# Output projection and MLP of a decoder step: unrolled, smaller weight groups, token scale applied to the relu output

## The reference, cut to what matters

```python
ob  = diff_head_norm(diff_attention(...), subln_gain, lambda_init)   # rmsnorm over 128 values of each head
mix = concatenate([oa, ob], axis=-1)                                 # 1024 per token
h   = x + mix @ w_out                                                # 1024 x 1024
u   = rmsnorm(h, norm_mlp) @ w_up                                    # 1024 x 4096
h   = h + square(relu(u)) @ w_down                                   # 4096 x 1024
y   = rmsnorm(h, final_norm)
```

## Time and profile before

| | us |
|---|---|
| runs (3): median, lowest, highest | 4612.5, 4608.19, 4615.78 |
| the profiled execution: span | 4601.9 |
| of it up to the stage `mlp` (its first transfer is issued at 2681.7) | 2681 |
| PE busy, share of the span | 4152.4, 90% |
| DVE | 2403.4, 52% |
| ACT | 1536.3, 33% |
| POOL | 805.8, 18% |

### The profile page before, as it was taken

One profiled execution on the slowest core, in us unless ns is written; L12 is line 12 of the kernel. 1 busy time (PEld: TensorE's weight loads), 2 busy tenths in 40 slices (PEclk: granted clock), 3 DMA queues, 4 the chain that ended last, 5 costly groups with the idle time before them and its releaser, 6 DMA issues. The chain is left out here.

```text
span 4601.9 us, 72420 instructions
## 1 busy us (share of the span) xinstructions
PE 4152.4 (90%) x22272; PEld 3160.3 (69%) x22272; DVE 2403.4 (52%) x5184; ACT 1536.3 (33%) x2569; POOL 805.8 (18%) x694
## 2 busy tenths in 40 slices
PE   7996998999989897888888879999999998999998
PEld 6875884445444444445444458988988997998898
DVE  3333334756677684444444435565565555555654
ACT  2221224555545443223322332233223223223322
POOL 0001000000000000333333322222222222222121
PEclk9997999999999998999999989999999999999999
DMA  5756623110111103999999953324333333332231
GB/s 187 234 194 211 228 76 86 36 37 8 36 35 37 36 10 114 376 330 350 365 348 349 360 171 120 116 95 128 127 100 113 124 110 103 125 118 99 94 125 61
DMA packets 347208, 686.79 MB, mean 149 GB/s; under 512 B 27769, under 2 KB 185465, under 8 KB 343610
## 3 DMA queue, kind: packets, MB, share of 16 engines
q1 hardware_dynamic: 291295, 448.03, 29.3%
q0 software_dynamic: 47488, 218.01, 13.3%
q10 hardware_dynamic: 8155, 17.77, 1.4%
HBM read 632.85 MB, written 117.70 MB: 163 GB/s over the span
## 5 line engine op out<-in xcount | busy, mean ns | idle before, releaser
L1379 POOL TENSOR_TENSOR d_up_lo<-d_up_raw,d_up_hi 128x2048 fp32r<-128x2048 f32 x100 | 460.6, 4606 | 1420.3 <-ACT d_up_hi L1516 1420.3
L1384 PE MATMUL d_ups<-d_a_hi,d_up_hi 128*128 128x416 f32 x1600 | 568.2, 355 | 16.9 <-DVE d_a_lo L1671 16.2
L1386 PE MATMUL d_ups<-d_a_hi,d_up_lo 128*128 128x416 f32 x1600 | 566.1, 354 | 0.0
L836 POOL DMA_DIRECT2D c_v<-in_v_cache x512 | 275.2, 537 | 1638.9 <-issue 1627.8
L1385 PE MATMUL d_ups<-d_a_lo,d_up_hi 128*128 128x416 f32 x1600 | 560.6, 350 | 0.0
L530 PE MATMUL b_s<-b_k,b_q 128*128 128x512 f32 (+3 forms) x1280 | 498.5, 547 | 54.1 <-DVE b_part L662 30.6
L1384 PE MATMUL d_dps<-d_u_hi,d_down_hi 128*128 128x416 f32 x1280 | 461.7, 361 | 57.6 <-DVE d_y L1696 55.8
L1696 DVE TENSOR_TENSOR d_y<-d_y,d_dps 128x416 f32<-128x416 f32 x640 | 367.9, 584 | 225.6 <-PE d_dps L1386 223.6
L1386 PE MATMUL d_dps<-d_u_hi,d_down_lo 128*128 128x416 f32 x1280 | 458.2, 358 | 0.0
L1385 PE MATMUL d_dps<-d_u_lo,d_down_hi 128*128 128x416 f32 x1280 | 454.0, 355 | 0.0
L530 PEld LDWEIGHTS b_s<-b_k,b_q 128*128 128x128 f32 x1280 | 236.6, 197 | 291.0 <-issue 191.1
(11 more groups left out here) (164 smaller groups left out, 6306.4 us busy)
## 6 DMA issues: line engine op xcount, KB each, us to landing
c_k<-in_k_cache SPq DMA_DIRECT2D x512, 256.0 KB, 6.2
c_v<-in_v_cache POOLq DMA_DIRECT2D x512, 256.0 KB, 5.7
d_down_raw<-in_w_down SPq DMA_DIRECT2D x80, 1024.0 KB, 5.1
d_up_raw<-in_w_up SPq DMA_DIRECT2D x80, 1024.0 KB, 7.3
out_ka_win<-in_ka_state POOLq DMA_DIRECT2D x8, 4064.0 KB, 14.6
out_va_win<-in_va_state POOLq DMA_DIRECT2D x8, 4064.0 KB, 26.5
d_up_raw<-in_w_out SPq DMA_DIRECT2D x20, 1024.0 KB, 7.5
a_x<-in_x_prompt SPq DMA_DIRECT2D x32, 512.0 KB, 4.1
```

The lines of the kernel that those rows point to most:

```text
L836: eng.dma_start(dst[i][:, g, :], io[src[0]][bass.ds(page, 1)].rearrange("o p d -> (o p) d")).then_inc(landed[i], 16)
L1379: nc.gpsimd.tensor_tensor(up_lo[i][:], up_raw[i][:], up_hi[i][:].bitcast(F32), ALU.subtract).then_inc(up_lo_ready, 1)
L1384: nc.tensor.matmul(dst, w_hi, x_hi, start=first, stop=False)
L1386: return nc.tensor.matmul(dst, w_lo, x_hi, start=False, stop=last)
```

## The change

All of `mlp` is straight code; no loop is left. In the new source the three matmuls are L1416 to L1418.

- Column groups of w_out and w_up are 128 wide (512 KB, rows of 512 bytes), with three buffers of `up_hi` and `up_lo` (UB). Groups are numbered through: 8 of w_out and 32 of w_up per block. Groups of w_down stay at 256 rows.
- `mix_hi`, `mix_lo` and `h_hi`, `h_lo` are separate. `mix` itself holds half a block at a time (4 chunks) and x a quarter. Mix and heads of the next block are prepared in groups MIX_AT = 3 and on and HEAD_AT = 8 and on.
- The up projection takes h times the gain. The token scale `per_token` = 1 / (mean square + eps) is the square of the norm's scale; DVE multiplies the relu output by it and then by the relu output. ACT makes the cast of u.
- POOL adds the squares of the 8 chunks (`add_square`), PE sums once (`sum_squares`) between the tiles up(0,0) and up(0,1).
- After a block each token tile of 104 is transposed, ACT squares it along its free dimension with an accumulated sum, and DVE multiplies by the token's scale and the gain row. SP stores.

On DVE, the end of a block before the change: down_lo and the split of group 15 stand ahead of the adds of group 14, head norms between them.

The diff, cut to its core:

```diff
-    GC = 256
-    NF = GC // P
-    OG, UG = D // GC, FF // GC
-    SG = OG + UG
+    NF = 2
+    OG, UG = KC, FF // (NF * P)
+    CG = OG + UG * NF
     NH = NP
-    DB = 3
+    UB, DB = 3, 3
+    XB = 2
+    MIX_AT, HEAD_AT, X_AT = 3, 8, 12
...
-        up_raw = [sb(f"d_up_raw{i}", [P, KC, GC]) for i in range(2)]
-        up_hi = [sb(f"d_up_hi{i}", [P, KC, GC], F32R) for i in range(2)]
-        up_lo = [sb(f"d_up_lo{i}", [P, KC, GC], F32R) for i in range(2)]
+        up_raw = [sb(f"d_up_raw{i}", [P, KC, P]) for i in range(2)]
+        up_hi = [sb(f"d_up_hi{i}", [P, KC, P], F32R) for i in range(UB)]
...
+                    b, s = n // CG, n % CG
+                    name, g = ("w_out", s) if s < OG else ("w_up", s - OG)
+                    src = io[name].rearrange("(c p) n -> p c n", p=P)[:, :, g * P:(g + 1) * P]
+                    sp.dma_start(up_raw[n % 2][:], src).then_inc(up_in[n % 2], 16)
...
+                    for c in range(KC):
+                        load_cols(out_no(b, c) + 2)
+                        if c % XB == 0 and 2 <= c // XB + 1 < KC // XB:
+                            load_x(b, c // XB + 1)
+                    for g in range(UG):
+                        load_cols(up_no(b, g, 0) + 2)
+                        load_rows(b, g)
+                        load_cols(up_no(b, g, 1) + 2)
...
-                        nc.gpsimd.tensor_tensor(up_lo[i][:], up_raw[i][:], up_hi[i][:].bitcast(F32),
-                                                ALU.subtract).then_inc(up_lo_ready, 1)
+                def cols_lo(n):
+                    if n >= NB * CG:
+                        return
+                    pool.wait_ge(up_hi_ready, n + 1)
+                    nc.gpsimd.tensor_tensor(up_lo[n % UB][:], up_raw[n % 2][:], up_hi[n % UB][:].bitcast(F32),
+                                            ALU.subtract).then_inc(up_lo_ready, 1)
...
+                    if c == 1:
+                        wait(pool, summed, b)
+                        nc.gpsimd.tensor_tensor(squares[:], square[:, 0, :], square[:, 1, :], ALU.add).then_inc(sq_added, 1)
+                    elif c > 1:
+                        pool.wait_ge(sq_added, b * (KC - 1) + c - 1)
+                        nc.gpsimd.tensor_tensor(squares[:], squares[:], square[:, c % 2, :], ALU.add).then_inc(sq_added, 1)
...
+                for b in range(NB):
+                    for c in range(KC):
+                        cols_lo(out_no(b, c) + 2)
+                        if c:
+                            add_square(b, c - 1)
+                    cols_lo(up_no(b, 0, 0) + 2)
+                    add_square(b, KC - 1)
...
-                def add_square(first, last):
-                    if first:
...
-                        pe.wait_ge(square_used, n)
-                        pe.sem_inc(s_full, 1)
...
+                def sum_squares(b):
+                    pe.wait_ge(sq_added, (b + 1) * (KC - 1))
+                    pe.wait_ge(head_rooted, (b + 1) * NH)
+                    nc.tensor.matmul(s_ps[:, 0:W], ones[:], squares[:], start=True, stop=True).then_inc(summed, 1)
...
-                        if c >= 2:
-                            add_square(c == 2, False)
-                    add_square(False, False)
-                    add_square(False, True)
-                    if b:
-                        for c in range(KC):
-                            add_square(c == 0, c == KC - 1)
...
-                    down(b, UG - 2, 0, (lambda c: c % 2 and add_square(True, True)) if b + 1 < NB else lambda c: None)
-                    down(b, UG - 1, 1)
...
+                    for g in range(UG + 1):
+                        if g < UG:
+                            up(b, g, 0)
+                            if g == 0:
+                                sum_squares(b)
+                            up(b, g, 1)
...
+                                    wait(pe, y_ready, 2 * y_no(b - 1, t))
+                                turn_y(b - 1, t, half, t_ps[half])
+                            if b < LAST and HEAD_AT < g <= HEAD_AT + NH and c == 4:
+                                sum_head(b + 1, g - HEAD_AT - 1)
+                        if g:
+                            down(b, g - 1, between)
+                pe.wait_ge(d_used, NB * UG * KC)
...
+                    act.wait_ge(up_in[n % 2], 16 * (n // 2 + 1))
+                    wait(act, u_full, n - UB + 1)
+                    nc.scalar.copy(up_hi[n % UB][:], up_raw[n % 2][:]).then_inc(up_hi_ready, 1)
...
-                def take_root(scale, which):
-                    n = sums.up()
-                    act.wait_ge(s_full, n)
-                    wait(act, root_used, n - 2)
-                    nc.scalar.activation(root[:, (n - 1) % 2, :], s_ps[:, 0:W], ACT.Sqrt, bias=eps[:, which:which + 1],
-                                         scale=scale).then_inc(rooted, 1)
...
+                def head_root(b, hd):
+                    n = b * NH + hd
+                    act.wait_ge(head_summed, n + 1)
+                    wait(act, headed, n)
+                    nc.scalar.activation(root[:], s_ps[:, 0:W], ACT.Sqrt, bias=eps[:, 1:2],
+                                         scale=1.0 / P).then_inc(head_rooted, 1)
...
+                def h_cast(b, c):
+                    n = b * KC + c
+                    act.wait_ge(h_ready, n + 1)
+                    nc.scalar.copy(h_hi[:, c, :], h[:, c % 2, :]).then_inc(h_hi_ready, 1)
...
+                    nc.scalar.activation(square[:, c % 2, :], y[b % 2][:, c, :], ACT.Square).then_inc(squared, 1)
...
+                def u_cast(b, g, f):
+                    n = u_no(b, g, f)
+                    act.wait_ge(u_ready, n + 1)
+                    wait(act, d_full, row_no(b, g) * KC - KC)
+                    nc.scalar.copy(u_hi[g % 2][:, f, :], u[:, f, :]).then_inc(u_hi_ready, 1)
...
+                    for half in range(2):
+                        act.wait_ge(y_turned, 2 * n + half + 1)
+                        if half == 0:
+                            wait(act, stored[n % 2], 16 * (n // 2))
+                        nc.scalar.activation(out[n % 2][:, half * 512:(half + 1) * 512], banks[half][0:TT, :], ACT.Square,
+                                             accum_out=own_sum[:, n % 2, half:half + 1]).then_inc(y_squared, 1)
...
+                    for g in range(UG):
+                        for f in range(NF):
+                            cols_hi(up_no(b, g, f) + 2)
+                            if g == 0 and f == 0:
+                                h_cast(b, KC - 1)
+                            if f == 0 and b and 2 <= g < 2 + TB:
+                                y_square(b - 1, g - 2, t_ps)
+                                y_root(b - 1, g - 2)
+                            if b < LAST and f == 0 and HEAD_AT + 1 < g <= HEAD_AT + 1 + NH:
+                                head_root(b + 1, g - HEAD_AT - 2)
+                            relus(b, g, f)
+                            if f == 0 and g:
+                                u_cast(b, g - 1, 1)
+                            if f == 1:
+                                u_cast(b, g, 0)
+                                rows_hi(b, g)
+                                if b < LAST:
+                                    if MIX_AT <= g < MIX_AT + NP:
+                                        mix_cast(b + 1, g - MIX_AT)
+                                    if HEAD_AT <= g < HEAD_AT + NH:
+                                        head_square(b + 1, g - HEAD_AT)
+                                    if HEAD_AT + 2 <= g < HEAD_AT + 2 + NH:
+                                        mix_cast(b + 1, NP + g - HEAD_AT - 2)
+                    u_cast(b, UG - 1, 1)
...
+                    part = y[b % 2][:, c, :]
+                    dve.wait_ge(x_copied, n + 1)
+                    dve.wait_ge(u_full, out_no(b, c) + 1)
+                    nc.vector.tensor_tensor(part, part, u_ps[c % 2][:, 0:W], ALU.add).then_inc(out_added, 1)
+                    dve.wait_ge(out_added, n + 1)
+                    if c < 2:
+                        wait(dve, u_split, b * UG * NF)
+                    else:
+                        dve.wait_ge(h_split, n - 1)
+                    nc.vector.tensor_scalar(h[:, c % 2, :], part, gain_mlp[:, c:c + 1], None, ALU.mult).then_inc(h_ready, 1)
...
+                def token_scale(b):
+                    dve.wait_ge(summed, b + 1)
+                    link(nc.vector.tensor_scalar(per_token[:], s_ps[:, 0:W], 1.0 / D, EPS, ALU.mult, ALU.add))
+                    nc.vector.reciprocal(per_token[:], per_token[:]).then_inc(scale_ready, 1)
...
+                def split_u(b, g, f):
+                    n = u_no(b, g, f)
+                    part = u[:, f, :]
+                    dve.wait_ge(relued, n + 1)
+                    if g == 0:
+                        dve.wait_ge(h_split, (b + 1) * KC)
+                    else:
+                        dve.wait_ge(u_split, n - NF + 1)
```

(48 more changed lines are left out.)

587 lines of the change are left out of this document (252 added, 335 removed).

## The result

The changed kernel takes 4808.1 us (median of 4 runs, 4802.3 to 4824.9) against 4610.3 us for the kernel before in the same series (4606.4 to 4615.8): a ratio of 1.0435, interval 1.0416 to 1.0454. It is 4.3% slower, where I had forecast 4471.9 us and given "slower" a chance of 0.04. The profiled execution has a span of 4806.1 us and a time of 4808.0, so only 1.9 us lie around the span and not the 10 us that I had named; the 10.6 us between the span and the median before are a difference between executions.

The account below looks back on a forecast made before the run. TensorE, full in mid-block, was taken as the bound, leaving only stalls, norms, start and tail to win. From 4612.5 us, -175.8 + 45.8 - 1 - 9.6 = -140.6 gave 4471.9 us, range 4440 to 4505.

Parts of the forecast that it names:

- Weight supply: Out projection loads, 512 KB with 512-byte rows: landings up to about 6.2 us cost nothing; cost put at 0.
- Rival 1: Plain up/down groups: GpSimd goes ahead of VectorE, up to 1.2 us in 59 more groups; 4543 us, chance 0.10.
- Rivals 2 and 3: Slow weight landing: above 6.2 us, 4528 at 9 us, chance 0.07; from about 12.5 us, 4632, chance 0.03.
- Rival 3: Per-load price slows out projection by 140 us; ScalarE's cast delays the seam to up by 20; 4632, chance 0.03.
- period of a block: First transpose to first transpose of the next block: 377.5 less 40.1 removed plus 10.0 added, 347.4 us.
- gaps at the last down group: Each block's end: TensorE waits for VectorE's adds and down_lo, 3.2 us x 5 = 16 us added.
- clock behind these gaps: Lower TensorE clock after each block's last down group gap: 0.8 us x 5 = 4 us added.
- head groups, GpSimd beside VectorE: Groups with a head: VectorE's multiplications wait for GpSimd, delaying u; 4.2 us a block, four blocks, 16.8 us added.
- seam out to up: Casts and rests of h chunks 6 and 7 come late for TensorE; 0.9 us x 5 = 4.5 us added.
- from the last add to the end: Tail of the stage after the last down: about 19 us instead of 28.6, a gain of 9.6 us.
- first out tile done after the stage's first transfer, against before: Start of the stage: first out tile ends 1 us earlier, bounds -4 and +4.
- the first head starts some 6 us later: Start: more bytes ahead of the last constant and ScalarE's first casts delay the first head some 6 us.

Follow-up runs that it names:

- load order mended: Changed kernel with SP issuing the second column load ahead of the row load in each up/down group; 4477.0 us, ratio 0.9714.
- the edit of the last group: On the changed kernel with ScalarE's second column cast behind relu and u cast: last group's down_lo halved between the preceding group's adds; 4440.4 us.
- GpSimd held back: Changed kernel with only GpSimd's subtraction of the second column tile held until the first half's rest of u is written; 4587.4 us, ratio 0.9957.

## Why the prediction was wrong

**The step that failed is "Weight supply ... I put 0".** The term was not too small; it left out who stands behind the load and behind the wait. In its place the runs show 331 us (4808.1 - 4477.0) from a late issue and a cast ahead of the relu. It has three faults.

- It worked out its bound, a landing of up to 6.2 us, in the out projection alone, where no row load is in the queue. There it held: w_out lands in 4.4 us, w_up in 7.1 (medians).

```profile
d_up_raw<-in_w_up SPq DMA_DIRECT2D x160, 512.0 KB, 7.1
...
d_up_raw<-in_w_out SPq DMA_DIRECT2D x40, 512.0 KB, 4.4
```

- It asked how long a load takes and not when it is issued. In the new order of SP the second column load, whose buffer was free at 2862.9 in the group above, stands behind a load that waits for down_lo until 2869.8. The diff shows the three lines together; I costed each edit on the engines that compute and did not walk SP's queue.
- It asked how long TensorE could do without the weights and not who stands behind the waiting cast. TensorE never waited for these weights. ScalarE did, with the relu behind it. Before, SP had the same order. SP and ScalarE in block 0 of the kernel before:

```profile
2860.74 0.37 SPq L1320 DMA_DIRECT2D d_down_raw<-in_w_down  x1
2861.45 0.37 SPq L1314 DMA_DIRECT2D d_up_raw<-in_w_up  x1
```

```profile
2865.76 1.90 ACT L1516 CAST d_up_hi<-d_up_raw 128x2048 fp32r<-128x2048 f32 x1
...
2883.89 1.90 ACT L1516 CAST d_up_hi<-d_up_raw 128x2048 fp32r<-128x2048 f32 x1
```

The load issued at 2861.45 is not the one that the cast at 2865.76 reads; by the source it is read by the cast at 2883.89, 22.4 us after its issue, and such a load lands in a median of 7.3 us. That made the order harmless, and the cast stood behind the second relu besides. The change kept the order of the loads and the number of raw buffers, two, but halved the column group, so the buffers reach half as far ahead: the load issued at 2870.22 is asked for at 2872.47 (2876.74 - 4.27), 2.3 us later. And it put one cast directly ahead of each relu. A third raw buffer would attack the short lead by itself; no run here tries it.

**Rival 1 named the right collision by the wrong road.** I gave a margin of 0.2 us in the plain groups and a chance of 0.10. The late cast released GpSimd and the relu together, so the margin was gone in nearly all of them (74 gaps). Its price was 1.2 us a group; with the lateness and the clock it was 4.4 us (331 / 75). **Rivals 2 and 3** priced a slow landing through TensorE's supply, from 6.2 or 12.5 us on; neither was the mechanism. Rival 3 did name a weight cast that waits on ScalarE and holds what stands behind it, but at the seam to up alone and only for a slow landing.

**The rest of the sum held in the main, in part because errors cancelled.** With the two lines swapped the kernel takes 4477.0 us, 5 us over the 4471.9. Against the kernel before in its own series (4607.5) that is 130.5 us less, where I had 140.6. Term by term:

| term | predicted | measured |
|---|---|---|
| period of a block | 347.4 | 348.3 (load order mended) |
| gaps at the last down group | 16 | 14.4 (9.1 of them removed by the edit of the last group) |
| clock behind these gaps | 4 | about 7 (the 48 matmuls take 10.4 to 10.5 us in all five, 9.0 where the clock stays up; load order mended) |
| head groups, GpSimd beside VectorE | 16.8 | 12.5 |
| down(0), GpSimd beside VectorE | nothing | 7.3 |
| seam out to up | 4.5 | 2.4 |
| from the last add to the end | 19 | 18.0 (4478.4 - 4460.4, load order mended) |
| first out tile done after the stage's first transfer, against before | -1 | +2.2 (43.8 against 41.7); +3.1 with the load order mended |

Heads and down(0) nearly cancel. The rows that ran over (start, clock, down(0)) and those that ran under leave some 4 to 5 of the missing 10 us unexplained. In the start, "the first head starts some 6 us later" was low: the square of the first head begins 22.9 us after the first transfer (2709.46) and began at 11.7 before (2693.46), 11.1 us later. The last constant came 3.7 of them later, and half a mix was still to be loaded after it. That the first tile was only 2.2 us later is partly luck: more was saved between first head and first tile than I had counted.

The Trainium skill (SBUF — State Buffer, SBUF: two separate sides) says that a VectorE operation with two SBUF inputs and a GpSimd operation that reads SBUF each take the shared ports for a whole instruction, and that the other blocks. The traces agree: 2.47 us beside a subtraction, 0.59 alone, and the adds, which read PSUM as their second input, never over 0.59:

```profile
L1738 DVE TENSOR_TENSOR d_y<-d_y,d_dps x640: 576/586/590, 2792.9 to 4788.1; 128x416 f32<-128x416 f32 x160
```

## What to carry to other kernels

When a diff writes the order of loads anew, walk the issuing engine's queue line by line: for each load, which wait stands ahead of it that it doesn't need itself. Then walk each engine that waits for a load and ask what stands behind that wait, even if the weights themselves are wanted much later. Smaller loads in the same number of buffers also shorten the time between issue and use (22.4 us before, 2.3 after). If down_lo, load, relu, adds and down_lo close a ring, compare the ring with the matmuls of a period (22.9 against 18.1 us here): a margin on one engine says nothing about it.

## What was not expected of the hardware

- Halving a GpSimd instruction saved VectorE almost nothing (2.92 against 3.06 us for two multiplications): each half won the turn ahead of the next VectorE operation.
- The clock cost more than I had put for such gaps. In the changed kernel, with gaps of 2.8 us and more, it fell behind 58 of 74. With GpSimd held back it fell behind none of the 63 gaps of up to 1.8 us, behind 3 of 5 between 1.9 and 2.3 us and behind 5 of 6 longer ones. Taking 141 us out of the gaps took 78 us out of the matmuls as well. What decides between two gaps of equal length, such as the two of about 3 us above, no run here shows.
